# Delta rule in a hybrid encoder: the two lower levels of a blockwise inverse and the state update computed in 64-column quadrants

## The reference: what must be computed

```
L = strict lower part of (beta*k) k^T * decay
A = L + I
u = A^-1 (beta*v)         w = A^-1 (beta*k*exp(gc))
v_new = u - w @ state
o     = (q*exp(gc)) @ state + attn @ v_new
state = state*exp(g_last) + k_dec^T @ v_new
```

## Time and profile before

| | |
|---|---|
| time, median of three | 1104.63 us |
| the profiled execution's own time | 1104.05 us |
| its span, first to last instruction | 1102.3 us |
| TensorE busy | 1053.3 us (96%) |
| VectorE busy | 528.6 us (48%) |
| mean granted TensorE clock | 0.989 |

### The profile page before, as it was taken

One profiled execution on the slowest core, in us unless ns is written; L12 is line 12 of the kernel. 1 busy time (PEld: TensorE's weight loads), 2 busy tenths in 40 slices (PEclk: granted clock), 3 DMA queues, 4 the chain that ended last, 5 costly groups with the idle time before them and its releaser, 6 DMA issues.

```text
span 1102.3 us, 14281 instructions
## 1 busy us (share of the span) xinstructions
PE 1053.3 (96%) x5878; PEld 884.9 (80%) x5878; DVE 528.6 (48%) x745; ACT 378.4 (34%) x563; POOL 124.0 (11%) x199
## 2 busy tenths in 40 slices
PE   8899999989998998999999999989999999999995
PEld 7789798767777888887888888878888888888884
DVE  5774445566657777455433515463333332322314
ACT  5444644654332212343322322252323232311212
POOL 4000000614663331000000000000000000000000
PEclk9999999999999999999999999989999999999998
DMA  9313320000010012213232326323333333233201
GB/s 299 112 48 115 102 80 1 1 1 11 3 18 12 1 40 77 78 39 97 94 115 65 126 77 225 91 67 94 98 102 90 110 82 115 77 115 105 94 11 76
DMA packets 104000, 87.18 MB, mean 79 GB/s; under 512 B 13109, under 2 KB 93697, under 8 KB 103936
## 3 DMA queue, kind: packets, MB, share of 16 engines
q1 hardware_dynamic: 102288, 81.80, 24.6%
q0 software_dynamic: 1488, 4.40, 1.1%
q10 hardware_dynamic: 160, 0.07, 0.0%
HBM read 83.64 MB, written 2.62 MB: 78 GB/s over the span
## 4 chain that ended last, share of the span: by engine, by line
PE 84%; DVE 8%; issue 3%; ACT 2%; POOL 2%; DMA 1%; SPq 0%; DVEq 0%; POOLq 0%; ACTq 0%
PE psum L887 22%; PE psum L888 22%; PE psum L889 22%; PE psum L1015 3%; PE psum L1033 3%; PE psum L1023 2%; PE psum L1285 1%; PE psum L1241 1%; PE psum L1214 1%; PE psum L1166 1%; DVE Zx L1876 1%; PE psum L1297 1%; PE psum L1271 1%; POOL Zs L796 1%; DMA x_tok<-in_x_dram 1%
## 5 line engine op out<-in xcount | busy, mean ns | idle before, releaser
L887 PE MATMUL psum<-hT_hi,w_hi 128*128 128x512 f32 (+1 forms) x712 | 279.6, 393 | 7.2 <-DVE w_lo L1876 5.5
L888 PE MATMUL psum<-hT_lo,w_hi 128*128 128x512 f32 (+1 forms) x712 | 278.3, 391 | 0.0
L889 PE MATMUL psum<-hT_hi,w_lo 128*128 128x512 f32 (+1 forms) x712 | 278.1, 391 | 0.0
L1876 DVE TENSOR_TENSOR w_lo<-w_raw,w_hi 128x2048 fp32r<-128x2048 f32 (+2 forms) x81 | 167.5, 2068 | 229.4 <-ACT w_hi L1454 229.4
L1454 ACT ACTIVATE w_hi<-w_raw 128x2048 fp32r<-128x2048 f32 (+2 forms) x82 | 141.4, 1724 | 163.9 <-PE psum L889 151.7
L887 PEld LDWEIGHTS psum<-hT_hi,w_hi 128*128 128x128 f32 (+1 forms) x712 | 134.1, 188 | 37.4 <-DVE w_lo L1876 6.8
L889 PEld LDWEIGHTS psum<-hT_hi,w_lo 128*128 128x128 f32 (+1 forms) x712 | 133.9, 188 | 28.6
L888 PEld LDWEIGHTS psum<-hT_lo,w_hi 128*128 128x128 f32 (+1 forms) x712 | 134.0, 188 | 28.1
L1876 DVE TENSOR_TENSOR psum<-gate_act,psum 128x512 f32<-128x512 f32 x22 | 15.3, 696 | 120.3 <-PE psum L889 120.3
L887 PE MATMUL psum<-w_hi,act_hi 128*128 128x512 f32 x176 | 68.5, 389 | 0.0
L888 PE MATMUL psum<-w_lo,act_hi 128*128 128x512 f32 x176 | 68.5, 389 | 0.0
(11 more groups left out here) (297 smaller groups left out, 1611.7 us busy)
## 6 DMA issues: line engine op xcount, KB each, us to landing
w_raw<-in_w_in_dram SPq DMA_DIRECT2D x23, 1024.0 KB
w_raw<-in_ffn_w_gate_up_dram SPq DMA_DIRECT2D x44, 512.0 KB
w_raw<-in_ffn_w_down_dram SPq DMA_DIRECT2D x10, 1024.0 KB
w_raw<-in_mem_w_kv_dram SPq DMA_DIRECT2D x4, 1024.0 KB
w_raw<-in_w_out_dram SPq DMA_DIRECT2D x4, 1024.0 KB
x_tok<-in_x_dram SPq DMA_DIRECT2D x4, 512.0 KB, 5.3
w_raw<-in_w_branch_mla_dram SPq DMA_DIRECT2D x4, 512.0 KB
w_raw<-in_w_branch_dn_dram SPq DMA_DIRECT2D x4, 512.0 KB
```

The costliest lines, as they stand in the source:

```text
L887: pe.matmul(o, s_hi, m_hi, start=first, stop=False)
L888: pe.matmul(o, s_hi, m_lo, start=False, stop=False)
L889: return pe.matmul(o, s_lo, m_hi, start=False, stop=last)
L1876: return dve.tensor_tensor(o, a, b, op)
```

## The change

Levels 4 and 5 are issued like level 6, as 64x64 quadrants, but those on the diagonal: `SAME` pairs each half with itself. All 16-, 32- and 64-blocks that these levels join lie within the diagonal quadrants; the off-diagonal ones are no longer written, and the mask of the next step sets them to zero. Each 128x128x128 product becomes two of 64x64x64. `scan_update` computes only the two diagonal blocks of each head pair: each 128x128x128 product becomes two with all 128 partitions contracted and 64x64 results, the first into partitions 0 to 63, the second into 64 to 127. A helper `turn_halves` replaces two loops with the same transposes. No instruction changes its place between its neighbours, no wait and no semaphore changes, and the other engines' lists are the same.

```diff
         HALVES = [(slice(0, 64), slice(64, P)), (slice(64, P), slice(0, 64))]
+        SAME = [(h, h) for h, _ in HALVES]
...
+            def turn_halves(key, p):
+
+                for j in range(4):
+                    m = pe.transpose(bank(key)[:, j * P:(j + 1) * P], Zs[:, p, j, :], ident[:, :])
+                return m
...
                     claim(pe, key)
                     for j in range(4):
-                        if s == LEVELS - 1:
-                            for near, far in HALVES:
-                                m = pe.matmul(bank(key)[far, j * P + near.start:j * P + near.stop], LT[g][near, p, j, far],
-                                              Xm[near, p, j, near], start=True, stop=True)
-                        else:
-                            m = pe.matmul(bank(key)[:, j * P:(j + 1) * P], LT[g][:, p, j, :], Xm[:, p, j, :], start=True,
-                                          stop=True)
+                        for near, far in HALVES if s == LEVELS - 1 else SAME:
+                            m = pe.matmul(bank(key)[far, j * P + near.start:j * P + near.stop], LT[g][near, p, j, far],
+                                          Xm[near, p, j, near], start=True, stop=True)
                     m.then_inc(full(key), 1)
...
                     for j in range(4):
-                        if s == LEVELS - 1:
-                            for near, far in HALVES:
-                                m = pe.matmul(bank(key)[far, j * P + near.start:j * P + near.stop], T1[near, p, j, far],
-                                              Zm[near, p, j, near], start=False, stop=(j == 3), skip_group_check=True)
-                        else:
-                            m = pe.matmul(bank(key)[:, j * P:(j + 1) * P], T1[:, p, j, :], Zm[:, p, j, :], start=False,
-                                          stop=False, skip_group_check=True)
+                        for near, far in HALVES if s == LEVELS - 1 else SAME:
+                            m = pe.matmul(bank(key)[far, j * P + near.start:j * P + near.stop], T1[near, p, j, far],
+                                          Zm[near, p, j, near], start=False, stop=(s == LEVELS - 1 and j == 3),
+                                          skip_group_check=True)
                     m.then_inc(zc_step if s < LEVELS - 1 else full(key), 1)
...
                     pe.wait_ge(vdec_ready, 2 * g + d + 1)
                     for j in range(4):
-                        m = pe.matmul(bank(key)[:, j * P:(j + 1) * P], k_tok[:, t, j * P:(j + 1) * P],
-                                      vdec[:, d, j * P:(j + 1) * P], start=True, stop=True)
+                        for h, _ in HALVES:
+                            own = slice(j * P + h.start, j * P + h.stop)
+                            m = pe.matmul(bank(key)[h, own], k_tok[:, t, own], vdec[:, d, own], start=True, stop=True)
                     m.then_inc(full(key), 1)
```

More of the change, by code:

```diff
@@ L1195, in first_inverse @@
                     pe.wait_ge(z0_ready, 2 * g + p + 1)
-                    for j in range(4):
-                        m = pe.transpose(bank(key)[:, j * P:(j + 1) * P], Zs[:, p, j, :], ident[:, :])
+                    m = turn_halves(key, p)
                     m.then_inc(full(key), 1)
```

## The result

The changed kernel took 1111.91 us (median of 20 runs, 1101.74 to 1113.82), the kernel before 1106.19 us (20 runs, 1102.88 to 1107.92) beside it. The ratio is 1.0045, 95% interval 1.003 to 1.0061: slower by about half a percent, where 0.65% faster was forecast. One thing is needed to read these numbers: the changed kernel's runs have two clusters, 3 of 20 at 1101.7 to 1104.0 us and 17 at 1108.8 to 1113.8, with a mean granted clock of 0.980 to 0.984 in the three and of 0.969 to 0.977 in the others.

The account below looks back on a forecast made before the run. TensorE was the default limit (96% busy), but in the edited 124 us stretch it and VectorE take turns, neither saturated. Turn gains 2.2 + 2.2 + 1.4 + 1.4 = 7.2 us took 1104.6 to 1097.4 us, range 1093.8 to 1102.6.

Parts of the forecast that it names:

- rival B: Longer idle times at level 5 in turns 1 to 3 each drop the clock: 4.8 us lost, 1102; chance 0.06.
- the sum: Gains of the edited stages over the four turns add to 7.2 us; update and switching taken as zero net.
- Its price: Cost of one clock drop, 1.6 us, read from the single drop before line 1271 and the projections after it.
- The stages: Products of levels 4 and 5: each stage 0.78 us shorter; turns 0 to 3 gain 2.2, 2.2, 1.4, 1.4 us.
- Level 4 of turns 2 and 3: Both products end earlier by 1 us or so under VectorE's cover, and nothing reads them sooner: zero gain.
- The update: scan_update, three times: about 58 ns an instruction, no change; worth +0.1 to -2.6 us, taken as 0.
- Rival C: Diagonal quadrants at levels 4 and 5 do not overlap: a stage takes 3.6 us, about 20 us lost, 1125; chance 0.06.
- Rival A: Level 5's gain is lost to another wait, or every switch of form drains: 4 us lost, 1101.4; chance 0.13.
- the drain: Changing tiling mode drains the engine, a whole matmul latency twice a stage: some 4 us over ten stages, leaving 3.

Follow-up runs that it names:

- run with half the heads: Kernel before, full products only, with products of two of four heads left out at level 4 of turns 2 and 3: 1108.27 us, ratio 1.0024.
- 28 pairs: Changed kernel with 28 pairs of unused 64x64x64 products filling the idle time ahead of level 5 in turns 2 and 3: 1100.36 us, ratio 0.9971.
- level 4 alone: Changed kernel with quadrants kept only at level 4, level 5 and the update in full form: 1105.84 us, ratio 1.0003.
- the mix: Changed kernel with level 4 of turns 2 and 3 in full form again: 1099.15 us, ratio 0.9942.
- the filled kernel: Changed kernel plus eight unused 128x128x128 products ahead of level 5 in turns 2 and 3: 1099.47 us, ratio 0.9956.
- all idle times filled: Changed kernel plus unused full products ahead of level 5 (turns 2, 3), before turn 1's first transposes and between scan_keys and scan_queries: 1097.87 us, ratio 0.9930.

## Why the prediction was wrong

- **The failed step** is rival B, the falling clock: the sum took the clock as unchanged, at no cost, and left its fall to a rival with 0.06 of the chance and 4.8 us. It is what happened, and the prediction's own sign of being wrong, a clock under 1 between 318 and 440 us, is there. I foresaw the idle time (about 2 us; measured 1.81 and 1.80) and wrote that 2 us "is nearer" to the 1.02 us that did not drop the clock than to the 3.31 us that did. That was interpolation between two points, taken as evidence. The run with half the heads shows falls behind 1.78 us, and three of the kernels with fillings have one behind 1.21 us, where the same wait a turn later had none. The length of one idle time does not decide it.
- **Its price** was off too: 1.6 us a fall was read where full projections follow the idle time. That price is right for such a place (the half-head kernel: 3 us over two falls, 1108.27 against 1105.27). Behind level 5's quadrants it is 7.0 us a turn: quadrants and `scan_values` follow, and both run at half speed. I had not asked what stands behind the idle time, nor that the change itself puts quadrants there.
- Turn 1 had a short fall as well (clock 0.59 at 344 to 348 us), under VectorE's cover; the turn still gained 2.1. It began in the attention products (line 1167, 1.88 us for 1.16), which follow the same waits of 1.35 and 0.48 us for GpSimd in the kernel before, there at full clock. Rival B named turn 1 too, for the wait ahead of T; the profile with 28 pairs has a long fall right there.
- **The stages** were right. Terms 2.2, 2.2, 1.4 and 1.4; measured 2.0, 2.1 and, with the clock held, 1.42 for turn 2. Level 4 of turns 2 and 3 gains nothing: with level 4 alone, turn 2 ran 32.90 us (second products at 378.99 and 411.89) against 32.91. With the idle time filled the whole came to 1099.5 against 1105.1, and with the mix to 1099.2 against 1105.3: 5.6 and 6.1 us of the 7.2. Where the rest goes is not shown; the mix's profiled execution, the fastest of its six at 1095.74 us, is 8.3 us below the profiled one of the kernel before, and has falls at 340 and 436 us all the same.
- **The update** was mis-sized: 58 ns an instruction taken, measured 34, the lower bound (1.08 us from 369.21 to line 1167 at 370.29). As forecast it is worth nothing, VectorE being the later one: 1.0003 alone. Part 3 of "TensorE: Matmul & The Clock Gate" in the Trainium skill, by which weight loads overlap only across row groups, would have let me expect no overlap of two tiles that share all rows; the trace has 34 ns for them as for the quadrants, so here the measurement decides against that reading.
- **Rival C** (diagonal quadrants do not overlap) is refuted: 32 of them take 1.08 us at full clock, as off the diagonal. **Rival A** and the drain of "TensorEngine Tiling (Array Packing)", Key Properties, in the Trainium skill, read as a full latency for each change, would have left 3 us of gain; the filled turn 2 shows none of that loss (1.42).

What stays open: which quantity makes the clock fall and brings it back, and why three runs of twenty of the changed kernel escaped most of it (their clocks of 0.980 to 0.984 are near those of the filled kernel, 0.982 to 0.988; none of the three is profiled). The execution matters, not only the program: with level 4 alone the clock fell in one turn and not in the next, at the same idle time.

## What to carry to other kernels

A saving on TensorE that only lengthens its wait for another engine is not neutral: look at how long the new idle time is and at what stands behind it. Shorten products where they end something, and leave them in full form under another engine's cover; put the dense work directly behind a wait (here 1100.4 against 1111.6 us). When a rival's price is read from one event, check that the same kind of work follows in the place where it would be paid.

## What the runs showed of the hardware

- The clock can stay at half speed while TensorE is busy without a break: 0.50 from 352 to 368 us, busy for 3.98 to 4.00 us of each 4 (filling with 28 pairs); 32 float32 instructions with 64 moving columns took 7.09 us in a row (3.7 at full clock). In the changed kernel, with one wait of 1.2 us within, both long falls ended in or right behind the transposes that follow line 1269 (1.91 and 1.32 us, 1.09 at full clock).
- The same wait in the same kernel can be followed by a fall or not: 1.80 and 1.81 us (level 4 alone), 1.21 us twice (all idle times filled).
- Eight unused 128x128x128 products, or 60 quadrant instructions, in 1.8 us of idle time saved 7 us a turn: unneeded work turned a loss of 5.7 us against the kernel before (1111.91, 1106.19) into a gain of 5.6 (1099.47, 1105.12).
- Two float32 tiles of 128 rows and 64 columns, side by side, go at 34 ns an instruction, like 64x64 ones.
